# Reordering the first block between the value projection and the sparse attention of a two-block kernel

## What is computed

```python
proj = rms_norm(h) @ w_in                       # hq hf hi hg | nq kc vc ks vs kw vw | ngate
o_hg  = hgrn2_mixer(hq, hf, hi, hg)             # 4 heads: gated recurrence over chunks, head norm, gate
kc = compress(k_cmp); vc = compress(v_cmp)      # silu(flat @ w1) @ w2, 31 compressed rows
kc = rope(rms_norm(kc, k_gain[0]), cmp_end)
o_cmp = softmax(q kc^T) vc                      # branch 1, compressed keys
o_slc, o_swa = attention(ks, vs), attention(kw, vw)   # branches 2 and 3, causal
o_nsa = g0 * o_cmp + g1 * o_slc + g2 * o_swa    # gates from ngate
h = h + concat(o_hg, o_nsa) @ w_out
h = h + ffn(rms_norm(h))
```

## Time and profile before

| | us |
|---|---|
| median of 3 runs | 2733.97 (2733.3 to 2739.57) |
| time of the profiled execution | 2727.69 |
| its span, first to last instruction | 2725.8 |
| PE busy in the span | 2457.3 (90%) |
| from PE's first `v0` matmul to the first score, layer 1 | 56.29 |
| the same in layer 2 | 56.28 |

### The profile page before, as it was taken

One profiled execution on the slowest core, in us unless ns is written; L12 is line 12 of the kernel. 1 busy time (PEld: TensorE's weight loads), 2 busy tenths in 40 slices (PEclk: granted clock), 3 DMA queues, 4 the chain that ended last, 5 costly groups with the idle time before them and its releaser, 6 DMA issues.

```text
span 2725.8 us, 35663 instructions
## 1 busy us (share of the span) xinstructions
PE 2457.3 (90%) x12328; PEld 1783.8 (65%) x12328; DVE 1166.9 (43%) x1889; ACT 642.7 (24%) x1238; POOL 1119.3 (41%) x766
## 2 busy tenths in 40 slices
PE   6989899999989888999999989999988889888885
PEld 5868667888867777677888868777676533333332
DVE  5685774212346866763213363324564521111113
ACT  4333462111013315551110022122312211111111
POOL 5662205666756741125666755342245011111110
PEclk9999899999999999999999999999999789999997
DMA  4112102233322112012232322221123379999996
GB/s 142 57 47 88 45 2 85 94 98 97 96 78 77 55 47 85 25 40 85 93 100 93 119 76 85 86 77 39 32 70 147 119 286 404 410 407 402 408 410 273
DMA packets 78167, 373.34 MB, mean 137 GB/s; under 512 B 11232, under 2 KB 11360, under 8 KB 53344
## 3 DMA queue, kind: packets, MB, share of 16 engines
q1 hardware_dynamic: 71904, 360.23, 36.6%
q0 software_dynamic: 5280, 8.40, 1.0%
q10 hardware_dynamic: 864, 3.15, 0.3%
HBM read 368.06 MB, written 12.58 MB: 140 GB/s over the span
## 4 chain that ended last, share of the span: by engine, by line
PE 68%; DMA 13%; DVE 13%; issue 3%; POOL 2%; ACT 1%; SPq 0%; DVEq 0%; POOLq 0%; ACTq 0%
PE PS L1992 16%; PE PS L1993 15%; PE PS L1994 15%; DMA arena<-w_up 12%; PE PS L2574 4%; PE PS L2379 2%; PE PS L2406 2%; PE PS L2471 2%; PE PS L2055 1%; PE PS L2362 1%; PE PS L2601 1%; PE PS L2393 1%; PE PS L2042 1%; DVE arena L1241 1%; POOL arena L646 1%
## 5 line engine op out<-in xcount | busy, mean ns | idle before, releaser
L622 POOL TENSOR_SCALAR whi<-ring 128x1024 fp32r<-128x1024 f32 x256 | 290.0, 1133 | 1034.4 <-PE PS L1994 862.6
L625 POOL TENSOR_TENSOR wlo<-ring,whi 128x1024 fp32r<-128x1024 f32 x256 | 647.3, 2528 | 21.3
L1993 PE MATMUL PS<-xl,whi 128*128 128x512 f32 x1376 | 541.9, 394 | 0.0
L1992 PE MATMUL PS<-xh,whi 128*128 128x512 f32 x1312 | 527.8, 402 | 15.0 <-POOL wlo L625 6.8
L1994 PE MATMUL PS<-xh,wlo 128*128 128x512 f32 x1312 | 515.7, 393 | 0.0
L2574 PE MATMUL PS<-arena,xraw 128*64 128x512 f32 x512 | 255.1, 649 | 59.7 <-DMA arena<-w_up 58.7
L1993 PEld LDWEIGHTS PS<-xl,whi 128*128 128x128 f32 x1376 | 262.2, 191 | 52.9 <-issue 3.4
L1992 PEld LDWEIGHTS PS<-xh,whi 128*128 128x128 f32 x1312 | 249.1, 190 | 70.5 <-issue 11.1
L1994 PEld LDWEIGHTS PS<-xh,wlo 128*128 128x128 f32 x1312 | 248.9, 190 | 52.8
L2575 PE MATMUL PS<-arena,xraw 128*64 128x512 f32 x512 | 256.2, 652 | 0.0
L2574 PEld LDWEIGHTS PS<-arena,xraw 128*64 128x64 f32 x512 | 71.3, 148 | 207.7 <-issue 206.1
(11 more groups left out here) (457 smaller groups left out, 4188.2 us busy)
## 6 DMA issues: line engine op xcount, KB each, us to landing
ring<-ring_w SPq DMA_DIRECT2D x280, 512.0 KB, 3.5
arena<-w_gate SPq DMA_DIRECT2D x64, 1024.0 KB, 25.2
arena<-w_up SPq DMA_DIRECT2D x64, 1024.0 KB, 27.4
xraw<-w_down SPq DMA_DIRECT2D x32, 1024.0 KB, 29.1
arena<-w_down SPq DMA_DIRECT2D x30, 1024.0 KB, 29.1
arena<-y_dram SPq DMA_DIRECT2D x8, 512.0 KB, 7.2
xT<-xT_in SPq DMA_DIRECT2D x2, 1024.0 KB, 6.6
out<-arena SPq DMA_DIRECT2D x4, 512.0 KB, 2.6
```

What stands on the lines that cost most here:

```text
L622: nc.gpsimd.tensor_scalar(hi, ring[:, t % RING, :], 1.0, 0.0, ALU.mult, ALU.add).then_inc(sems["whi"], 1)
L625: nc.gpsimd.tensor_tensor(wlo[:, t % RING, :], ring[:, t % RING, :], hi, ALU.subtract).then_inc(sems["split"], 1)
L1992: mm(out, a[0], b[0], start=start, stop=False, skip_group_check=skip_group_check)
L1993: mm(out, a[0], b[1], start=False, stop=False, skip_group_check=skip_group_check)
```

## The change

It moves steps in the three tables, splits the compression's first weight into eight steps of one tile each (`cmpt0` to `cmpt7`, PE), and moves three things into the attention:

- PE: `v1` follows `v0`. `cmpt0` to `cmpt3` (keys) stand between the `state` steps, `cmpt4` to `cmpt7` (values) around the `hn` steps. `rs6` stands behind the scores of item 0 and `rr6` behind those of item 4. The list of waits at the attention's start is broken up: each item waits for the queries and keys that it uses, items from 8 on for `kcr`, the first product for `VC`.
- ACT: `feat19` stands ahead of `gatem0`, `qs0` to `qs2` ahead of `hi3`, then `v1`, `ket`, `ks0`. `cmph0` stands behind `hn1`, `cmph1` behind `hn3`. The four `wh` instructions go one by one behind the exps of items 1 to 4, `rs6` behind item 1.
- DVE: `dbuild1` follows `dbuild0`; the low parts `ql` and `kl` come before `hn0`. `cmpo`, `rs6` and `rr6` run in the attention at items 1, 2 and 6. The low parts of the heads come with items 2 to 5 (before: 0 to 3).
- The out parts start with item 4 (before: item 2). Some banks and buffers change so that the moved work does not collide.

```diff
@@ buffers, out parts
-        Pr8 = Pr + (ftmp[:, 0, :], ftmp[:, 1, :], qgn[:, 0, :], qgn[:, 1, :], qgn[:, 2, :])
+        Pr8 = (ftmp[:, 0, :], ftmp[:, 1, :], rrs[:, 1, :], qgn[:, 1, :], qgn[:, 3, :], rrs[:, 0, :], lnb, qgn[:, 0, :])
...
-            n = (it["k"] if it else 0) - 2
+            n = (it["k"] if it else 0) - 4
@@ ACT, attend_nsa
+                    if 1 <= s <= 4:
+                        act_e.wait_ge(sems["hn"], nth("hn", l, s))
+                        nc.scalar.activation(woh[s - 1], mixT[:, s - 1, :], ACT.Identity).then_inc(sems["wh"], 1)
+                    if s == 1:
+                        step(l, "rs", 6)
@@ DVE, attend_nsa
-                        if k < 4:
+                        if s == 1:
+                            step(l, "cmpo", 0)
+                        elif s == 2:
+                            step(l, "rs", 6)
+                        elif s == 6:
+                            step(l, "rr", 6)
+                        if 2 <= s < 6:
@@ PE, compression tile by tile
-                elif kind == "cmph":
+                elif kind == "cmpt":
...
-                    else:
+                    elif i == 4:
                         pe.wait_ge(sems["gates"], nth("gates", l, 1))
-                    pe.wait_ge(sems["dbuild"], nth("dbuild", l, i + 1))
+                    kv, q = i // 4, i % 4
+                    if q == 0:
+                        pe.wait_ge(sems["dbuild"], nth("dbuild", l, kv + 1))
+                    pe.wait_ge(sems["split"], nth("split", l, T_CMP + i + 1))
+                    for pr in range(4 * q, 4 * q + 4):
@@ PE, attention
-                    pe.wait_ge(sems["hrs"], nth("hrs", l, 4))
-                    pe.wait_ge(sems["ql"], nth("ql", l, 4))
-                    pe.wait_ge(sems["kl"], nth("kl", l, 2))
-                    pe.wait_ge(sems["vcc"], nth("vcc", l, 1))
-                    pe.wait_ge(sems["rope"], nth("rope", l, 7))
@@ PE, nsa_scores and attend_nsa
+                if k < 8 and k % 2 == 0:
+                    pe.wait_ge(sems["ql"], nth("ql", l, k // 2 + 1))
+                if k in (0, 10):
+                    pe.wait_ge(sems["kl"], nth("kl", l, k // 10 + 1))
+                if k == 8:
+                    pe.wait_ge(sems["rope"], nth("rope", l, 7))
...
+                    if s == 0:
+                        step(l, "rs", 6)
+                    elif s == 4:
+                        step(l, "rr", 6)
@@ PE_STEPS, ACT_STEPS, DVE_STEPS
-    "hi3 rr5 v0 ket0 ket1 ket2 state0 gatet0 state1 v1 state2 state3 cmph0 hn0 hn1 cmph1 hn2 hn3 cmpo0 rs6 "
-    "rr6 attention0 wout0 norm1 ffn0")
+    "hi3 rr5 v0 v1 ket0 ket1 ket2 state0 gatet0 cmpt0 state1 cmpt1 state2 cmpt2 state3 cmpt3 cmpt4 hn0 cmpt5 hn1 "
+    "cmpt6 hn2 cmpt7 hn3 cmpo0 attention0 wout0 norm1 ffn0")
-    "rs3 decay3 feat17 feat18 scan3 gatem0 rs4 rs5 hi3 feat19 qs0 ket0 ket1 ket2 state0 qs1 state1 qs2 state2 v1 "
-    "gatet0 state3 ks0 qs3 hn0 hn1 cmph0 ks1 cmph1 hn2 hn3 cmpo0 rs6 wh0 attention0 norm1 ffn0")
+    "rs3 decay3 feat17 feat18 scan3 feat19 gatem0 rs4 rs5 qs0 qs1 qs2 hi3 v1 ket0 ket1 ket2 ks0 state0 gatet0 qs3 "
+    "state1 ks1 state2 state3 hn0 hn1 cmph0 hn2 hn3 cmph1 cmpo0 attention0 norm1 ffn0")
-    "gram10 gram11 gram12 gram13 gram14 gram15 rs4 rr3 qk2 qk3 rs5 rr4 dbuild0 rr5 ql0 state0 state1 ql1 dbuild1 "
-    "ql2 state2 hn0 kl0 hn1 ql3 kl1 hn2 hn3 rs6 cmpo0 rr6 attention0 wout0 norm1 ffn0")
+    "gram10 gram11 gram12 gram13 gram14 gram15 rs4 rr3 qk2 qk3 rs5 rr4 dbuild0 dbuild1 rr5 ql0 ql1 ql2 "
+    "state0 state1 kl0 state2 ql3 kl1 hn0 hn1 hn2 hn3 attention0 wout0 norm1 ffn0")

```

More of the change, by code:

```diff
@@ L860, in step @@
                         act_e.wait_ge(sems["hn"], nth("hn", l, 4))
-                    src = PS[:, 6, 0:n] if i < 6 else PS[:, 1, 256:256 + n]
+                    src = PS[:, 6, 0:n] if i < 6 else PS[:, 5, 256:256 + n]
                     nc.scalar.activation(lnb[:, 0:n], src, ACT.Ln, bias=eps[:, 0:1]).then_inc(a_ch, 1)
@@ L924, in step @@
                     nc.scalar.activation(rrs[:, i % 2, :], lnb[:, :], ACT.Exp, scale=-0.5).then_inc(sems["hrs"], 1)
-                elif kind == "wh":
-                    for k in range(4):
-                        act_e.wait_ge(sems["hn"], nth("hn", l, k + 1))
-                        nc.scalar.activation(woh[k], mixT[:, k, :], ACT.Identity).then_inc(sems["wh"], 1)
                 elif kind == "attention":
@@ L1267, in step @@
                         v.wait_ge(sems["dbuild"], nth("dbuild", l, 2))
-                    src = PS[:, 7, 0:n] if i < 6 else PS[:, 1, 384:384 + n]
+                    src = PS[:, 7, 0:n] if i < 6 else PS[:, 5, 384:384 + n]
                     nc.vector.tensor_tensor(gtmp[:, 0:n], src, sn, ALU.mult)
@@ L1290, in step @@
                         ins = nc.vector.tensor_copy(VC[rows, :, j, :],
-                                                    PS[rows, 0, P:2 * P].rearrange("p (g d) -> p g d", d=64))
+                                                    PS[rows, 6, P:2 * P].rearrange("p (g d) -> p g d", d=64))
                     ins.then_inc(sems["vcc"], 1)
@@ L2065, in step @@
                     pe.wait_ge(sems["rrstd"], nth("rrstd", l, i))
-                    dst = PS[:, 6, 0:n] if i < 6 else PS[:, 1, 256:256 + n]
+                    dst = PS[:, 6, 0:n] if i < 6 else PS[:, 5, 256:256 + n]
                     mm(dst, ones_64, sq2[:, i % 2, 0:n], start=True, stop=True).then_inc(sems["stat"], 1)
@@ L2071, in step @@
                     pe.wait_ge(sems["rope"], nth("rope", l, i))
-                    dst = PS[:, 7, 0:n] if i < 6 else PS[:, 1, 384:384 + n]
+                    dst = PS[:, 7, 0:n] if i < 6 else PS[:, 5, 384:384 + n]
                     mm(dst, rotm, qnb[:, i % 2, 0:n], start=True, stop=True).then_inc(sems["rot"], 1)
@@ L2102, in step @@
                             of = 2 * CMP_N * hc
-                            ins = mm(PS[:, 1 - i, of:of + 2 * CMP_N],
-                                     ring[:, t % RING, (pr % 4) * 256 + hc * P:(pr % 4) * 256 + hc * P + P],
+                            w = (pr % 4) * 256 + hc * P
+                            ins = mm(PS[:, 1 - kv, of:of + 2 * CMP_N], ring[:, (T_CMP + i) % RING, w:w + P],
                                      rhs, start=(pr == 0 and hc == 0), stop=(pr == 15), skip_group_check=True)
-                        if pr % 4 == 3:
-                            ins.then_inc(sems["tile"], 1)
+                    ins.then_inc(sems["tile"], 1)
                 elif kind == "cmpo":
@@ L2399, in pv_pair @@
                 qt, first = one["qt"], one["k"] % NSA_QT == 0
+                if one["k"] == 0:
+                    pe.wait_ge(sems["vcc"], nth("vcc", l, 1))
                 if first and qt >= 2:
```

13 lines of the change are left out of this document (5 added, 8 removed).

## The result

| | before | with the change |
|---|---|---|
| median, us | 2733.64 (2726.34 to 2742.28, 6 runs) | 2714.30 (2707.43 to 2719.54, 6 runs) |
| ratio | | 0.9927, 95% interval [0.9907, 0.9946] |
| time of the profiled execution | 2727.69 | 2716.43 |
| its span | 2725.8 | 2714.6 |
| first `v0` to the first score, layers 1 and 2 | 56.29, 56.28 | 49.09, 49.03 |

The forecast was 2724.8 (2717 to 2733). The kernel became 19 us faster, not 9. The two profiled executions are only 11.3 apart, though. Where this difference comes from turned out to be the main question of this case.

The account below looks back on a forecast made before the run. PE, busy 90% of the span, was taken as the bound, so only its idle or low-clock time could be won. Per layer -7.8 + 1.3 + 1.9 = -4.6, two layers -9.2: median 2724.8, range 2717 to 2733.

Parts of the forecast that it names:

- A: From the first `v0` to the first attention score: 7.8 us less per layer, bounds 6.3 and 8.8.
- B: Attention's entry: moved work on ACT, DVE and PE plus a postponed out part, 1.3 us more per layer.
- C: Low PE clock from `cmpo` to about item 4: 1.9 us more per layer, bounds 0 and 3.5.
- The postponed out part: Attention's entry: four out parts instead of five done by item 8's scores, 0.8 us more per layer.
- The rest of the program shifts with it: Behind the two attention entries: block 2 and the experts' loads only move earlier, leaving 9.2 us less in all.
- The clock stays high: Attention's entry: no low-clock cost, 6.5 us less per layer, 13 in all, 2721; chance 0.2.
- ACT's switches cost more: Three table switches before `cmpo` each cost another load, 3.8 us less gain per layer, 2732.4; chance 0.07.
- Paid back in the attention: First ten items each delayed 0.3 us, out parts find no gap: 4.6 us more per layer, 2731; chance 0.17.
- The low clock holds: Attention's items: PE's clock stays low until item 14, 10 us more per layer, 2744; chance 0.07.

Follow-up runs that it names:

- gap_filled_before: Kernel before with nine matmuls of no use in PE's wait at `rr6`, no step moved: 2720.45 us, ratio 0.9946.
- after_look_3: Changed kernel, unchanged, run once more for its trace: 2722.69 us.
- before_look_1: Kernel before, unchanged, run once more for its trace: 2733.15 us.
- before_again: Kernel before, unchanged, against itself, for its scatter and a second trace: 2734.31 us, ratio 0.9995.

## Why the prediction was wrong

**The order of events was right.** The first score was forecast at 280.0 and came at 280.86, `cmpo` at 278.1 and 278.35, its wait 3.2 and 3.13, the wait at `hn3` 0.5 and 0.45; `state3` waits for nothing. Item 8 was forecast near 293 and came at 292.11. The clock was to be 0.50 from 281 to 290 and was so from 280 to 288.

**Terms A to C.** A was -7.8 with `cmpo` at the high clock; the first score came 7.2 earlier with `cmpo` at the low one, which costs 0.64 (278.35 to 280.86 is 2.51 instead of 1.87), so A alone is -7.8. For the way from the first score to item 8, B and C had +1.0 together; the mean of the traces is 11.5 against 10.4, +1.1. Oversized was the price of `cmpo` at the low clock, put at 1.4. Up to item 8 the forecast was 2 x (-7.8 + 0.5 + 1.9) = -10.8, and 12.2 is the difference of the traces' means (66.4 and 67.0 before, 60.7 and 60.5 after).

The postponed out part, put at 0.8, seems to be missing at first sight, as the rest of the attention takes 109.1 with the change and 107.9 to 110.7 before. But these have different clocks. Where the rest of before has no low clock (as shown, layer 1, and gap_filled_before) it takes 107.9 or 108.0, and with the change it has none either and takes 109.1, PE being busy for 101.3 instead of 100.7. So some 1.1 us per layer are paid here, about what B supposed; that they are the out part was not isolated. The window in after_look_3, to be set beside 298.40:406.30 above:

```profile
292.40:401.50 109.10, 101.31 (x856) 75.83 (x855) 81.98 (x241) 66.49 (x182) 10.26 (x6) 1.00 0.05 16
```

**The step that failed is "The rest of the program shifts with it", and with it the 9.2 us set off against the median.** The sum had no term for anything but the entry of the two attentions, and took the 6.3 us between the traced execution and the median for an offset that the change leaves alone. By the traces' means (five and six):

| us | forecast | measured |
|---|---|---|
| `v0` to item 8, both layers | -10.8 | -12.2 |
| from there on, up to block 2's attention | +1.6 | +0.6 |
| ahead of the first `v0`, and from block 2's attention on | 0 | -2.5 |
| all that was traced | -9.2 | -14.1 |
| all executions | -9.2 | -18.4 |

The section that the sum describes was thus missed by 2.4 us (11.6 instead of 9.2), and 6.8 of the 9.2 us by which the forecast is off lie outside it, or in executions that were not traced. Nor did the rest of that section simply shift. Against the trace I had, the change gains 11.9 up to the items 8 and gives back 1.2 in layer 1's attention, 3.1 on the way to layer 2 and 2.9 behind it: 1561.8 became 1557.4. Against the other four it keeps its gain: 1570.1 became 1557.4. Four of the five traces of before have low clock behind the gap that the fifth has less of (3.4 and 10.2 us in the rest of the two attentions of three of them, 37.5 on the way to layer 2), and the change has less of it too (0, 0 and 30.7). Yet what lies behind the items 8 takes as long with the change as there (1436.4 us, and 1436.9 in before_look_1): what the clock gives, the change pays back elsewhere in it. That the clock behind the gap has a price at all, which the sum left out, gap_filled_before shows: -14.6 with no step moved, 4.2 of it up to the items 8.

**The rivals.** *The clock stays high* didn't happen (0.50 from 280 to 288). It was nearer in time (2721), but by luck, as it took the clock of the entry alone. *ACT's switches cost more* falls: each silu starts 0.02 us after its load's end, as 271.82 after 270.52 + 1.28. By that, the drain of about 1380 ns that the Trainium skill gives in "ScalarE: Activation LUTs", section "What ACT_TABLE_LOAD costs", doesn't show here either; the load agrees. *Paid back in the attention* falls by its size: it wanted 3.3 us per layer on top of the 3.2 of B and C, and all that was paid is 2.8 (0.64, 1.1 and 1.1 as above). *The low clock holds* falls: 1.00 from 290 on.

**What stays open.** All eleven traces of the table together give 2732.7 for before (five) and 2718.6 with the change (six), 14.1 apart, where the pooled executions are 18.4 apart. Which executions happened to be traced can account for such a difference (standard errors of 2 to 2.5 us on each side), but the shortest ones of before (2719 to 2725) and of the change (2707 to 2709) were not traced, and what they do otherwise was not seen. A pointer is the pair of kernels with the cross attention filled: they are 11.5 ± 2.0 apart, which is the 11.6 that the traces give for the section from the first `v0` to block 2's attention. By this the other 6.9 would lie in the cross attention. But its traced lengths differ by 1.4 only (means 28.0 and 26.6), so it is not shown.

Layer 2's way to block 2 takes 599.4 with the change and 596.4 before, in every trace. About half of these 3 us is the clock right ahead of block 2's attention: PE is busy throughout in both, with the clock at 0.58 in the change and at 1.00 in before_again, and does 14 instructions instead of 22:

```profile
1774.00:1778.00 4.00, 4.00 (x14) 3.35 (x14) 0.58 (x2) 0.81 (x4) 1.22 (x1) 0.58 0.14 58
```

```profile
1788.00:1792.00 4.00, 4.00 (x22) 3.36 (x21) 0.49 (x2) 0.81 (x4) 1.30 (x1) 1.00 0.16 67
```

Why the clock falls there with the change was not found, nor where the other half goes.

## What to carry to other kernels

- An empty stretch of PE can cost more than its length. Ask what the granted clock does in it and behind it, and try it: matmuls of no use in the gap give that price without any reordering. Here they gave 14.6 us, where a careful new order gives 18.4. The two gains lie in different places, and filling the change's own shorter wait gave only 2.3 ± 1.3 more.
- Before a sum from one trace is set against a median, trace the unchanged kernel several times and cut each trace at the same instructions. Several stages had two or three lengths each (cross attention 19.6, 24.7, 30.2; ahead of the first `v0` 228.9, 231.6, 234.5), and a single trace shows one of them. Compare a stage's length only where the granted clock is the same: the 1.1 us that the change costs in the rest of the attention are hidden otherwise. With a scatter of 5 us a difference of a few us needs dozens of executions, or a comparison by stages.
- A faster start is worth little if the next queue is the limit: one pair of table loads brought the first score 4 us forward and item 8 by one.

## What the hardware showed that I had not expected

- The time of one unchanged kernel ranges over 24 us (2719.1 to 2743.1), and it goes with the clock: 0.31 us for each us of low clock, correlation 0.89. The low stretches fall at other places of the same program from one execution to the next, and the durations come in steps, not as a continuum: the rest of the attention took 107.9 with no low clock in it, 109.0 with 3.4 us of it and 110.7 with 10.2.
- A stretch of low clock seems to bring others with it far behind. In the one trace with the gap of layer 1 filled, the way from that attention to layer 2, whose code and inputs are the same, takes 615.7 with 27.3 us of low clock, where four of five traces without the fill have 620.7 and 37.5. The fifth has 615.7 too, so that one trace alone proves nothing; the mean of 11 executions, 14.6 us lower where the two stretches save 4.2, speaks for it.
